# Seven-product part of an encoder kernel: VectorE's 128x2048 subtractions as two of 128x1024 each

## The chip, the cores and the metric

One core of a Trainium2 chip runs the whole kernel. The metric is the device time of one execution in microseconds (us). Three executions of the kernel before took 3186.99, 3185.45 and 3185.02 us; the median is 3185.45 us.

## The reference, cut to what matters

The model is an encoder of two layers over two sequences of 16 meta tokens and 512 tokens, with 1024 channels: one attention mixer, one state-space mixer, and a feed-forward block behind each. The change lies in the second feed-forward block:

```
def swiglu(u, w_gate, w_up, w_down):
    return (jax.nn.silu(u @ w_gate) * (u @ w_up)) @ w_down
# u = rmsnorm(h, ffn_norm[layer]);  h = h + swiglu(u, ...)
# w_gate, w_up: 1024 x 2816, w_down: 2816 x 1024, all float32
```

## The kernel before, in words

Every float32 product is made of three products of the shorter type fp32r: high part by high part, high weight by low token part, and low weight by high token part. A low part is the exact value minus the high part. The high part is a copy into fp32r.

The gate and up products of the second feed-forward block are cut into 2x2 blocks: two halves of the 1024 input channels (4 tiles of 128 each, `KH` = 4), two tiles of 128 outputs, and two halves of the tokens (512 each). For all but the first two tiles of gate and up, seven block products are made in place of eight (Strassen's scheme in Winograd's form). Each takes 4 x 3 = 12 matmuls of 128x128 by 128x512. The seven token operands are four plain or already turned halves and sums and differences of them; they are made once. The weight factors are made anew for each of the 20 pairs of output tiles (`PRODUCT_PAIRS`). The list `PRODUCTS` gives the order: (0,1), (0,2), (0,6), (0,5), (0,7), (1,1), (0,4), (0,3), (1,2), and so on; the first number is the pair and the second the product. We call them by their place in the list, t = 0, 1, 2, ...

The order on each engine is written out by hand, and semaphores tie the engines together:

- VectorE (DVE) makes the token operands: `first_difference` and `second_difference` per tile of 128x512; the third difference (line 3332) over 128x2048; the low parts of operands 2, 1 and 3 with `low_operand` (line 3267), 128x2048 each; `fourth_difference`, which is four steps of 128x512 (helper line 3241), a wait for the last of them, and one subtraction of 128x2048 (line 3262); two steps of the plain second hidden tile (lines 3340 and 3343, 128x1024); and the low part of operand 4 (line 3267 again). Behind them in its order stand the `take_quadrant` calls, which take finished products out of PSUM (lines 3277 and 3279).
- ScalarE (ACT) makes the high parts of the operands (`high_operand`, line 2353), the high parts of the weight factors (`high_factor`, line 2367), copies some products out of PSUM for later use (`tap`, line 2385) and applies silu (`quadrant_silu`, line 2390). Its order around t = 3 and 4 is: `high_factor(7)`, the high part of operand 4, silu of quadrant 0 of pair 0, `high_factor(8)`, `tap(4)`.
- GpSimd (POOL) makes the low parts of the weight factors (`low_factor`, line 999) and, ahead of the low factor of each product 6, four sums of weight quarters (`factor_sums`, lines 1006 to 1012). All are 128x512.
- TensorE (PE) runs `factor_product(t)`. It waits for the low factor t; for product 6, 5, 7 and 4 of pair 0 for `t_ready` 1, 2, 3 and 4, which the `low_operand` calls of VectorE give in that order; and for the taps (`tapped`) and the emptied banks (`quad_taken`). Product 4 of pair 0 (t = 6) needs `t_ready` 4 and `tap(4)`.
- SyncE (SP) issues the loads of the weight quarters, each when its old content has been used.

Of the kernel before, what the change touches and what calls it, by code (L numbers as in the profile page):

```python
# [22 lines left out]
F32 = mybir.dt.float32  # L23
F32R = mybir.dt.float32r
I32 = mybir.dt.int32
ALU = mybir.AluOpType
# [103 lines left out]
KH = KD // 2  # L130
# [193 lines left out]
def encoder(nc, tensors):  # L324
# [5 lines left out]
    def sb(name, shape, dt=F32, stack=None):  # L330
        return (stack or base).enter_context(nc.sbuf_tensor(name, shape, dt))
# [70 lines left out]
    with ExitStack() as s:  # L402
# [4 lines left out]
        with ExitStack() as s2:  # L407
            T1, T2, T3 = (sb(n, [P, 2, KH, SEQ], F32R, s2) for n in ("T1", "T2", "T3"))
        with ExitStack() as s2:
            TF1, TF2, TF3 = (sb(n, [P, 2, KH, SEQ], F32, s2) for n in ("TF1", "TF2", "TF3"))  # L410
# [103 lines left out]
    def real_half(ap, s):  # L514
        return ap[:, s * L + N_META:(s + 1) * L]

    def turned_half(ap):

        return ap[:, 0:KH, L + N_META:2 * L]
# [72 lines left out]
    b11_ready, t1_made, t2_made, t3_made = (Again(x, HEADS) for x in (k_hi, k_lo, q_hi, q_lo))  # L592
    t4_made, t_high = Again(q_turned, HEADS), Again(qs_ready, HEADS)
    t_ready, third_taken = Again(k_squared, HEADS), Again(kr_taken, HEADS)
# [1855 lines left out]
    def _(vec):  # L2450
# [59 lines left out]
        def step(ins):  # L2510

            ins.then_inc(vec_steps, c.adds(vec_steps))
            vec.wait_ge(vec_steps, c.given(vec_steps))
# [7 lines left out]
        for m in range(KQ + KKV):  # L2521
# [14 lines left out]
            if m >= KQ:  # L2536
                k = m - KQ
# [616 lines left out]
        for n in range(SCAN + 1):  # L3154
            i, k = divmod(n, CPS)
# [83 lines left out]
        def turned(dst, k, of, sub):  # L3239

            return vec.scalar_tensor_tensor(dst, of, col("ffn1", k), sub, ALU.mult, ALU.subtract)
# [13 lines left out]
        def fourth_difference():  # L3255

            f = turned_half(UF[1])
            vec.wait_ge(t_ready.sem, t_ready.at(1))
            for k in range(KH):
                ins = turned(f[:, k, :], KH + k, real_half(H[:, KH + k, :], 0), T2[:, 0, k, :].bitcast(F32))  # L3260
            step(ins)
            vec.tensor_tensor(f, f, T2[:, 1].bitcast(F32), ALU.subtract).then_inc(t4_made.sem, 1)

        def low_operand(n, hi, exact, lo):

            vec.wait_ge(t_high.sem, t_high.at(n))
            vec.tensor_tensor(lo, exact, hi.bitcast(F32), ALU.subtract).then_inc(t_ready.sem, 1)

        def take_quadrant(p, q):

# [22 lines left out]
        def add_down(m, g, final):  # L3293
# [35 lines left out]
        vec.sem_inc(third_taken.sem, 1)  # L3329
        vec.sem_inc(gate_ready, 1)  # L3330
        vec.wait_ge(t2_made.sem, t2_made.at(KH))
        vec.tensor_tensor(TF3[:, 1], TF2[:, 1], TF3[:, 1], ALU.subtract)\
            .then_inc(t3_made.sem, 1)
        low_operand(2, T2[:, 0], TF2[:, 1], T2[:, 1])
        low_operand(1, T1[:, 0], TF1[:, 1], T1[:, 1])
        low_operand(3, T3[:, 0], TF3[:, 1], T3[:, 1])
        vec.wait_ge(to_vector[0], c.want(to_vector[0]))
        fourth_difference()
        vec.wait_ge(plain_out.sem, plain_out.at(16))
        step(vec.tensor_tensor(hid_, real_group(0), rms, ALU.mult))  # L3340
# [200 lines left out]
```

## Time and profile before

| | |
|---|---|
| median of 3 executions | 3185.45 us |
| profiled execution | 3184.64 us |
| its span, first to last instruction | 3182.8 us |
| mean granted TensorE clock | 0.991 |
| PE busy | 3083.6 us, 97% |
| DVE busy | 1794.4 us, 56% |
| POOL busy | 1349.3 us, 42% |
| ACT busy | 916.5 us, 29% |

The span is the time between the first and the last instruction in the trace; 1.84 us of the profiled execution lie around it. Busy shares are averages over the whole span. A start in the rows is in us from the span's start, and durations include the time in which an instruction that has begun waits for something inside its engine.

### The profile page before, as it was taken

The page shows a single profiled execution, that of the slowest core. Times are in us where ns is not written, and L with a number is a line of the kernel's source. Part 1 is how long each engine was busy: PE and PEld are TensorE (multiplying, and loading weights), DVE is VectorE, ACT ScalarE, POOL GpSimd, SP SyncE. Part 2 cuts the span into 40 slices and gives each one's busy share as a digit, 9 for nine tenths or more (in the row PEclk, how much of TensorE's full clock was granted, in tenths as well). Part 3 has the DMA queues.
Part 4 walks back from the last instruction along what each step waited for, and adds up shares of the span by engine and source line. Part 5 has one row for each costly group of instructions (what it writes and reads, how often), then busy time and mean ns, then how long its engine had stood idle before and what let it go on. Part 6 is the DMA issues. An engine that isn't in the chain of part 4 may idle for free.

```text
span 3182.8 us, 46973 instructions
## 1 busy us (share of the span) xinstructions
PE 3083.6 (97%) x18566; PEld 2788.0 (88%) x18566; DVE 1794.4 (56%) x2496; ACT 916.5 (29%) x1628; POOL 1349.3 (42%) x710
## 2 busy tenths in 40 slices
PE   8999999899999999999999999899999899999997
PEld 8999999899999999999999988576667688887886
DVE  6677777643333333334788852588888833334334
ACT  4466665621000000001121122233334433332101
POOL 4100000133444444444444444467673577775442
PEclk9999999999999999999999999999999999999998
DMA  3011000121111111111243423332324122223221
GB/s 122 25 36 32 22 25 16 41 88 40 47 46 46 41 44 46 46 46 47 70 132 90 137 87 111 110 118 89 118 89 130 48 87 82 80 80 129 99 86 67
DMA packets 133065, 230.27 MB, mean 72 GB/s; under 512 B 10005, under 2 KB 59413, under 8 KB 132885
## 3 DMA queue, kind: packets, MB, share of 16 engines
q1 hardware_dynamic: 93136, 180.21, 16.7%
q10 hardware_dynamic: 39749, 47.60, 4.5%
q8 instruction: 121, 1.98, 0.3%
q14 instruction: 59, 0.48, 0.0%
HBM read 180.77 MB, written 46.99 MB: 72 GB/s over the span
## 4 chain that ended last, share of the span: by engine, by line
PE 84%; DVE 6%; POOL 5%; issue 4%; ACT 1%; DMA 0%; DVEq 0%; ACTq 0%; POOLq 0%
PE PS L1035 77%; PE PS L1289 4%; PE PS L1274 2%; POOL Wlo L915 1%; POOL SQ L960 1%; POOL RMS L925 1%; POOL SQ L955 1%; PE PS L1575 1%; DVE MX L2682 1%; DVE GD L3064 0%; POOL STB L947 0%; DVE XW L3026 0%; PE PS L1723 0%; DVE KAP L3069 0%; DVE YC L2931 0%
## 5 line engine op out<-in xcount | busy, mean ns | idle before, releaser
L870 POOL TENSOR_TENSOR Whi<-Wraw,const 128x1024 fp32r<-128x1024 f32 x145 | 354.7, 2446 | 1520.4 <-PE PS L1035 921.8
L1035 PE MATMUL PS<-Uhi,Whi 128*128 128x352 f32 (+1 forms) x2280 | 567.5, 341 | 17.1 <-DVE Ulo L2474 14.0
L1035 PE MATMUL PS<-Ulo,Whi 128*128 128x352 f32 (+1 forms) x2280 | 563.4, 339 | 0.0
L1035 PE MATMUL PS<-Uhi,Wlo 128*128 128x352 f32 (+1 forms) x2280 | 561.8, 339 | 0.0
L1035 PEld LDWEIGHTS PS<-Uhi,Whi 128*128 128x128 f32 x2280 | 395.0, 189 | 40.0 <-issue 17.4
L1035 PEld LDWEIGHTS PS<-Uhi,Wlo 128*128 128x128 f32 x2280 | 398.4, 189 | 20.8
L1035 PEld LDWEIGHTS PS<-Ulo,Whi 128*128 128x128 f32 x2280 | 397.6, 188 | 20.9
L873 POOL TENSOR_TENSOR Wlo<-Wraw,Whi 128x1024 fp32r<-128x1024 f32 x145 | 397.4, 2740 | 11.4
L1035 PE MATMUL PS<-T,Whi 128*128 128x512 f32 x768 | 225.7, 395 | 0.8 <-DVE HID L3285 0.5
L2815 DVE TENSOR_TENSOR H<-H,PS 128x1056 f32<-128x1056 f32 x88 | 110.3, 1253 | 130.7 <-PE PS L1035 130.6
L2931 DVE SCALAR_TENSOR_TENSOR YC<-XC,cols,YC 128x1052 f32<-128x1052 f32 (+1 forms) x96 | 180.8, 1884 | 3.4
L2682 DVE TENSOR_REDUCE MX<-PS 106x1 f32<-106x528 f32 x160 | 113.2, 707 | 113.0 <-PE PS L1035 112.3
L1035 PEld LDWEIGHTS PS<-T,Whi 128*128 128x128 f32 x768 | 143.8, 187 | 36.7 <-issue 0.9
L1289 PE MATMUL PS<-V,PT 106*106 106x64 f32 x1600 | 170.0, 254 | 0.5 <-ACT O L2017 0.5
L1289 PEld LDWEIGHTS PS<-V,PT 106*106 106x106 f32 x1600 | 161.8, 173 | 0.6 <-issue 0.6
L2112 ACT ACTIVATE HIDhi<-HID 128x1056 fp32r<-128x1056 f32 x20 | 21.8, 1088 | 457.1 <-DVE HID L2844 457.1
L2839 DVE TENSOR_TENSOR HID<-PS,RMS 128x1056 f32<-128x1056 f32 x22 | 27.7, 1258 | 217.7 <-PE PS L1035 217.4
L2006 ACT ACTIVATE PR<-PS,MX,TOK 106x528 f32<-106x528 f32 x160 | 126.5, 791 | 49.2 <-DVE MX L2685 48.9
L3296 DVE TENSOR_TENSOR H<-H,PS 128x1024 f32<-128x1024 f32 x47 | 57.4, 1220 | 141.3 <-PE PS L1035 141.3
L1035 PE MATMUL PS<-T,Wlo 128*128 128x512 f32 x384 | 136.0, 395 | 0.0
L999 POOL TENSOR_TENSOR Wlo<-Wraw,Whi 128x512 fp32r<-128x512 f32 x80 | 110.3, 1381 | 54.1 <-ACT Whi L2367 54.1
L1035 PE MATMUL PS<-YThi,Whi 128*128 128x512 f32 x256 | 120.7, 471 | 1.4 <-DVE Wlo L3151 0.8
(355 smaller groups left out, 6156.2 us busy)
## 6 DMA issues: line engine op xcount, KB each, us to landing
Wraw<-in_w SPq DMA_DIRECT2D x151, 512.0 KB, 3.2
Wraw<-in_w SPq DMA_DIRECT2D x152, 256.0 KB, 2.9
xt<-XTT ACTq DMA_DIRECT2D x20, 640.0 KB, 5.9
H<-in_x ACTq DMA_DIRECT2D x16, 528.0 KB, 8.3
zt<-ZB ACTq DMA_DIRECT2D x32, 256.0 KB, 2.1
X<-xt SPq DMA_DIRECT2D x8, 1024.0 KB
Z<-zt SPq DMA_DIRECT2D x32, 256.0 KB, 2.7
KFB<-keyf SPq DMA_DIRECT2D x15, 530.0 KB, 3.8
```

What stands on the lines that cost most here:

```text
L870: pool.tensor_tensor(Whi[s][:], Wraw[s][:], ones.unsqueeze(1).broadcast_to([P, BLK, P]), ALU.mult)\
L873: pool.tensor_tensor(Wlo[s][:], Wraw[s][:], Whi[s][:].bitcast(F32), ALU.subtract)\
L915: pool.tensor_tensor(Wlo[s][:], Wraw[s][:], Whi[s][:].bitcast(F32), ALU.subtract)\
L999: pool.tensor_tensor(OPLO[j % SLOTS], FACTOR[PRODUCTS[j][1]], OPHI[j % SLOTS].bitcast(F32), ALU.subtract)\
L1035: ins = pe.matmul(out, lhsT, rhs, start=start, stop=stop, skip_group_check=True)
L1274: ins = pe.transpose(PS[0:CW, A_TURN + b // TURN_DVE, b % TURN_DVE * CW:(b % TURN_DVE + 1) * CW], PR[t % 2][:, key_start(b):key_start(b) + ...
L1289: ins = pe.matmul(PS[0:CW, A_OUT, 0:VD], PT[t % 2][:, b, :], V[x // 4 % 2][:, n // KB * KB + b, x // 2 % 2, x % 2 * VD:(x % 2 + 1) * VD], ...
L2006: act.activation(PR[t % 2][:].rearrange("p (h n) -> p h n", h=2), PS[0:CW, A_SCORE:A_SCORE + 2, 0:QHALF], ACT.Exp, bias=MX[:, t % RING:t % ...
L2682: step(vec.tensor_reduce(MX[:, t % RING:t % RING + 1], PS[0:CW, A_SCORE:A_SCORE + 2, 0:QHALF], AX_XY, ALU.max))
L2815: ins = vec.tensor_tensor(h, h, of(g), ALU.add)
L2931: ins = vec.scalar_tensor_tensor(y_[:, :, to], x[:, :, of], taps[:, tap:tap + 1], y_[:, :, to], ALU.mult, ALU.add)
L3296: ins = vec.tensor_tensor(real(H[:, m, :]), real(H[:, m, :]), real_group(g), ALU.add)
```

## The change

Each of the five VectorE subtractions of 128x2048 becomes two of 128x1024. The first handles tiles 0 and 1 and the second tiles 2 and 3 of the four. The semaphore is given by the second. Nothing is moved, and no wait is added or removed.

```
         def fourth_difference():
             ...
             step(ins)
-            vec.tensor_tensor(f, f, T2[:, 1].bitcast(F32), ALU.subtract).then_inc(t4_made.sem, 1)
+            for k in range(0, KH, 2):
+                ins = vec.tensor_tensor(f[:, k:k + 2, :], f[:, k:k + 2, :], T2[:, 1, k:k + 2, :].bitcast(F32), ALU.subtract)
+            ins.then_inc(t4_made.sem, 1)
 
         def low_operand(n, hi, exact, lo):
             vec.wait_ge(t_high.sem, t_high.at(n))
-            vec.tensor_tensor(lo, exact, hi.bitcast(F32), ALU.subtract).then_inc(t_ready.sem, 1)
+            for k in range(0, KH, 2):
+                ins = vec.tensor_tensor(lo[:, k:k + 2, :], exact[:, k:k + 2, :], hi[:, k:k + 2, :].bitcast(F32), ALU.subtract)
+            ins.then_inc(t_ready.sem, 1)
...
-        vec.tensor_tensor(TF3[:, 1], TF2[:, 1], TF3[:, 1], ALU.subtract)\
-            .then_inc(t3_made.sem, 1)
+        for k in range(0, KH, 2):
+            ins = vec.tensor_tensor(TF3[:, 1, k:k + 2, :], TF2[:, 1, k:k + 2, :], TF3[:, 1, k:k + 2, :], ALU.subtract)
+        ins.then_inc(t3_made.sem, 1)
         low_operand(2, T2[:, 0], TF2[:, 1], T2[:, 1])
         low_operand(1, T1[:, 0], TF1[:, 1], T1[:, 1])
         low_operand(3, T3[:, 0], TF3[:, 1], T3[:, 1])
```

`low_operand` is called four times, so with the third and the fourth difference five instructions become ten.

## Rows read from the trace of the kernel before

**Rows 1.** The page: busy time of PE, and the chain's shares by engine.

```profile
PE 3083.6 (97%) x18566; PEld 2788.0 (88%) x18566; DVE 1794.4 (56%) x2496; ACT 916.5 (29%) x1628; POOL 1349.3 (42%) x710
PE 84%; DVE 6%; POOL 5%; issue 4%; ACT 1%; DMA 0%; DVEq 0%; ACTq 0%; POOLq 0%
```

**Rows 2.** Chain that ended last, 2480 to 2600: start us, us, what.

```profile
2502.79 0.50 POOL Wlo L999
...
2519.50 1.68 POOL OPS L999
...
2521.22 12.80 PE PS L1035 x48
2534.02 0.87 issue
```

**Rows 3.** Timeline of TensorE: start us, us, engine, line, what [idle before <-releaser].

```profile
2514.98 0.40 PE L1035 MATMUL PS<-Uhi,Wlo 128*128 128x512 f32 x1
2521.22 4.42 PE L1035 MATMUL PS<-T,OPS 128*128 128x512 f32 x12 [5.85 <-POOL OPS L999]
```

**Rows 4.** Timeline of GpSimd, 2502 to 2536.

```profile
2502.79 3.44 POOL L999 TENSOR_TENSOR Wlo<-Wraw,Whi 128x512 fp32r<-128x512 f32 x1 [13.54 <-ACT Whi L2367]
2509.49 3.35 POOL L1006 TENSOR_TENSOR S<-Wraw 128x512 f32<-128x512 f32 x1
...
2519.46 1.71 POOL L999 TENSOR_TENSOR OPS<-Wraw,OPS 128x512 fp32r<-128x512 f32 x1
2522.81 3.34 POOL L999 TENSOR_TENSOR Wlo<-Wraw,Whi 128x512 fp32r<-128x512 f32 x1
2526.10 3.54 POOL L999 TENSOR_TENSOR Wlo<-Wraw,Whi 128x512 fp32r<-128x512 f32 x2
2529.61 3.34 POOL L999 TENSOR_TENSOR OPS<-S,OPS 128x512 fp32r<-128x512 f32 x1
2534.39 1.28 POOL L999 TENSOR_TENSOR Wlo<-Wraw,Whi 128x512 fp32r<-128x512 f32 x1 [1.43 <-ACT Whi L2367]
```

**Rows 5.** Timeline of VectorE, 2498 to 2533.

```profile
2498.83 1.41 DVE L3241 SCALAR_TENSOR_TENSOR TF<-H,cols,TF 128x512 f32<-128x512 f32 x2
2500.16 1.23 DVE L3326 TENSOR_TENSOR HID<-HID,SILU 128x1024 f32<-128x1024 f32 x1
2501.31 1.22 DVE L3328 TENSOR_TENSOR GATE<-PS,RMS 128x1024 f32<-128x1024 f32 x1
2502.77 2.29 DVE L3332 TENSOR_TENSOR TF<-TF 128x2048 f32<-128x2048 f32 x1 [0.24 <-DVE GATE L3328]
2504.98 10.01 DVE L3267 TENSOR_TENSOR T<-TF,T 128x2048 fp32r<-128x2048 f32 x3
2514.91 6.80 DVE L3241 SCALAR_TENSOR_TENSOR UF<-H,cols,T 128x512 f32<-128x512 f32 x4
2521.75 3.25 DVE L3262 TENSOR_TENSOR UF<-UF,T 128x2048 f32<-128x2048 f32 x1
2524.92 1.21 DVE L3340 TENSOR_TENSOR HID<-PS,RMS 128x1024 f32<-128x1024 f32 x1
2526.28 2.21 DVE L3343 TENSOR_TENSOR HID<-HID,SILU 128x1024 f32<-128x1024 f32 x1
2528.64 3.16 DVE L3267 TENSOR_TENSOR Ulo<-UF,Uhi 128x2048 fp32r<-128x2048 f32 x1
2531.72 0.68 DVE L3277 TENSOR_TENSOR PS<-GATE,PS 128x512 f32<-128x512 f32 x1
```

**Rows 6.** Timeline of ScalarE, 2523 to 2535.

```profile
2523.75 1.15 ACT L2367 ACTIVATE Whi<-Wraw 128x512 fp32r<-128x512 f32 x2 [3.72 <-DMA Wraw<-in_w]
...
2526.69 1.91 ACT L2353 ACTIVATE Uhi<-UF 128x2048 fp32r<-128x2048 f32 x1
2533.16 0.63 ACT L2390 ACTIVATE GATE<-GATE 128x512 f32<-128x512 f32 x1 [4.56 <-DVE GATE L3279]
...
2534.22 0.58 ACT L2385 ACTIVATE SILU<-PS 128x512 f32<-128x512 f32 x1
```

**Rows 7.** Windows of 1 us: length, busy by engine, PEclk (granted clock), DMA.

```profile
2523.00:2524.00 1.00, 1.00 (x4) 0.71 (x3) 1.00 (x1) 0.25 (x1) 1.00 (x1) 0.50 0.11 41
2534.00:2535.00 1.00, 0.13 (x2) 0.14 (x2) 0.10 (x1) 0.79 (x2) 0.61 (x1) 1.00 0.00 0
```

**Rows 8.** Waits of TensorE from 2536 on: total us, times, longest.

```profile
PE PS L1035 <- DVEq L3382: 2.7, 1, 2.7
PE PS L1035 <- ACT SQ L2431: 1.1, 2, 0.6
```

## The prediction

> **What bounds the kernel now.** I read the page first. TensorE is busy for 97% of the span and carries 84% of the chain that ended last [rows 1], so a change to VectorE can only count where TensorE stands idle. The chain in order of time shows two such places near the edited lines. It leaves TensorE at about 2502.8, runs over GpSimd's low factors and sums until 2521.2, goes back to TensorE for 48 matmuls (t = 2 to 5), and has a hole of 0.87 us at 2534.0 which it calls "issue" [rows 2]. TensorE's timeline gives the first place its size: the last matmul of t = 1 starts at 2514.98 and lasts 0.40, and t = 2 starts at 2521.22, after 5.85 us of idleness that GpSimd's low factor 2 ended [rows 3].
>
> Next I read GpSimd and VectorE side by side, since both are busy without a break there. A GpSimd subtraction of 128x512 takes 1.28 us alone (at 2534.39) but 3.44, 3.35 and 3.34 us beside VectorE's 128x2048 instructions, and 1.71 beside its 128x512 ones [rows 4]. VectorE is slowed in turn: its first 128x2048 instruction takes 2.29 us, the three that follow 10.01 together; its 128x512 steps go from 1.41 for two to 6.80 for four, and a 128x1024 product of two SBUF tensors from 1.23 to 2.21 [rows 5]. The two take turns, one instruction each. From start to start, a 128x2048 instruction has 2504.98 - 2502.77 = 2.21 us alone and (2514.91 - 2504.98)/3 = 3.31 with a GpSimd turn in it, a 128x512 step about (2500.16 - 2498.83)/2 = 0.67 and 6.84/4 = 1.71. A GpSimd turn thus costs VectorE 1.04 to 1.10 us, whatever the size of its own instruction. VectorE's line 3340, which reads PSUM and one SBUF tensor, takes 1.21 beside GpSimd and was not held up [rows 4, 5].
>
> The Trainium skill, SBUF — State Buffer, "Who interferes with whom", says that a VectorE instruction with two SBUF inputs and a GpSimd instruction that reads SBUF exclude each other for a whole instruction, that one with a single SBUF input does not take part, and that it is the order of issue, not the shape, that decides who blocks. The trace agrees with the first two (2.29 against 3.31 us; line 3340 with 1.21). The advice in its summary to favour whichever side is on the critical path speaks against this change if VectorE is the later side; that is what the next step looks into.
>
> **The hole at 2534.0 is VectorE's.** Product t = 6 needs `tap(4)`, which is the ScalarE copy at 2534.22 of 0.58 us; it ends at 2534.80, and TensorE starts at 2534.89 (2534.02 + 0.87) [rows 2, 6]. That copy stands behind `high_factor(8)`, which stands behind the silu of quadrant 0 at 2533.16, which had waited 4.56 us for VectorE's line 3279 [rows 6]. Line 3279 and 3277 (start 2531.72) are `take_quadrant(0, 0)`, right behind the low part of operand 4 [rows 5]. From 2502.77 to 2531.72 VectorE runs without a gap over 0.15 us [rows 5]. So there are two gates: GpSimd's chain ends at 2521.2, VectorE's at 2531.7, and the second already ends last.
>
> **The change, gate by gate.** *GpSimd's gate (gain).* Seven GpSimd instructions lead to low factor 2: two low factors, four sums, low factor 2. Now they wait for the VectorE turns TF, three low operands and three 128x512 steps: 4 x 2.21 + 3 x 0.67 = 10.85 us. With halves they wait for seven half turns. A 128x1024 instruction alone takes 2501.31 - 2500.16 = 1.15 us from start to start [rows 5], so 7 x 1.15 = 8.05. Low factor 2 is ready 2.8 us earlier, at about 2518.4, and TensorE's idleness falls from 5.85 to about 3.0 us. The four products t = 2 to 5, of 12.80 us [rows 2], then end at about 2531.2 instead of 2534.0.
>
> *VectorE's gate (loss).* The halves give GpSimd more turns before VectorE is through. Before, ten VectorE instructions of this stretch hold a GpSimd turn: the three low operands, four 128x512 steps, the fourth difference, line 3343, and the last low operand (the long ones in rows 5). GpSimd has 12 instructions up to low factor 7; the other two are free, one beside line 3340, one (at 2529.61) after VectorE's last [rows 4]. With halves I lay them out again: turns behind TF's first half and so on, seven until low factor 2 (2518.4); low factor 3 before the first 128x512 step, 4 to 6 before the other three, 7 before the first half of the fourth difference. All 12 now fall on VectorE instructions with two SBUF inputs. Low factors 5 and 6 need quarters that are reloaded after low factor 2; now ScalarE has them at 2523.75 [rows 6], 2.6 us after 2521.2, so then at about 2521.0, in time for a turn at 2522.3. Low factor 7 needs t = 2 done, at about 2518.4 + 4.4 = 2522.8, in time for 2526. Low factor 8 can't come early: its high part stands behind the silu. So two more turns at 1.05 = 2.1 us. Each split costs 2 x 1.15 - 2.21 = 0.09, five times 0.45 us. VectorE's gate moves by 2.1 + 0.45 = 2.55 us, from 2531.72 to about 2534.3. The high part of operand 4 (1.91 us) is covered by lines 3340 and 3343, 1.36 + 1.15 = 2.51 us. Everything behind it (silu, `high_factor(8)`, `tap(4)`) follows, and t = 6 starts at 2534.89 + 2.55 = 2537.4.
>
> *TensorE's clock (loss).* TensorE then idles from 2531.2 to 2537.4, 6.2 us, where it idled 0.87 us. After the 5.85 us of idleness the granted clock was 0.50, that is 1.2 GHz, up to 2524 at least, and t = 2 took 4.42 us [rows 3, 7]; 12 matmuls at the full clock take (12.80 - 4.42)/36 x 12 = 2.8 us. That is 1.6 us lost. After 0.87 us the clock stayed at 1.00 [rows 7]. The first idleness still lasts 3.0 us and the clock may fall in it as before; its loss lies ahead of the second gate and is hidden. The new long one comes right ahead of t = 6, whose 1.6 us nobody hides.
>
> *Behind t = 6.* TensorE waits for nothing longer than 2.7 us until the end, and that at the final norm [rows 8]; GpSimd's next low factor hangs on ScalarE and moves along. The delay is passed on whole.
>
> Sum: 2.55 + 1.6 = 4.2 us slower. Against the profiled execution: 3184.64 + 4.2 = 3188.8. It was 0.8 us below the median of the three; on the median, 3185.45 + 4.2 = 3189.6 us. The gain of 2.8 us at the first gate is worth nothing, since the later gate moves the other way.
>
> Bounds. The number of added turns is 1 to 3 (a low factor that misses its turn and runs beside line 3340 is free; one more can't be excluded): 1.05 to 3.15 us. The split costs 0 (if the second half starts as if it were one instruction) to 0.45. The clock costs 0 to 1.6. So the mechanism gives +1.1 to +5.2.
>
> **Rivals.** (a) *Gain stays.* If t = 6 is not held by VectorE, the 2.8 us of the first gate are kept and the hole of 0.87 may close: 3181.8 to 3182.7 us. It decides if `take_quadrant(0, 0)` begins by 2531.72 - 3.7 = 2528.0. Half of the chain's view speaks for it: the profile names only the first gate and calls the second "issue". Against it: VectorE has no gap to give up, and splitting removes no work. (b) *The change doesn't do what it says.* Both halves may run with no GpSimd turn between them, as the second one is already queued when the first ends. Then GpSimd's turns stay, and the time is +0 to 0.45: 3185.7. Against it: today the three low operands are queued as closely, and a GpSimd turn stands between each two. (c) *Turns, but no clock loss*: 3185.45 + 2.55 = 3188.0. Against it stands the fall in 5.85 us of idleness. (d) *Something larger*: the reordered turns push a low factor behind its product in pair 1 as well, with another idle stretch and another 1.6 us: +7 or more, 3192.5 or later. GpSimd's low factor 9 is done about 1 us ahead of its product, but both move by the same amount.
>
> **How the numbers follow.** Forecast 0.58, (a) 0.12, (b) 0.12, (c) 0.13, (d) 0.05. The forecast alone spans 3187.5 to 3190.9. The range, 3184.8 to 3191.5, takes in (b) and (c) and leaves out (a) and (d). A change within 0.2% (6.4 us), about what a measurement of this kernel can tell from no change, is by far the likeliest, since all cases but (d) stay within it: slower by over 0.2% 0.05, faster 0.02, same 0.93.
>
> **What would show it.** Right: GpSimd's 128x512 instructions of about 2.3 us in place of 3.35 from 2503 on; TensorE idle about 3 us ahead of t = 2; line 3277 first at about 2534.3; TensorE idle some 6 us ahead of t = 6 and its first 12 matmuls at half the clock. Wrong: line 3277 at or before 2531.7, GpSimd durations as before, or a full clock at t = 6. A change of more than 6.4 us either way would mean that I missed a stage.

## The result, and the profile after

The changed kernel takes 3189.89 us (median of 20 executions, 3187.03 to 3195.63), the kernel before 3184.37 us in 20 executions beside it. The ratio is 1.0018, with a 95% interval of 1.0012 to 1.0024: slower by about 5.5 us (3.8 to 7.6). The forecast was 3189.6 us, 4.2 us slower. In one later set of runs three executions of the kernel before took 3498 to 6131 us; they are left out of its median there.

All times below that are "from the third difference" count from the start of its first instruction. This takes out what earlier stages add by chance: that start lay at 2502.77 us before, 2505.21 in the profile after, and 2502.43 in another profile of the same changed kernel. The profiled execution after has a span of 3190.4 us, so it shows 7.6 us more than before, of which 2.44 lie ahead of the edited lines.

VectorE's timeline of the changed kernel answers to [rows 5]:

```profile
2505.21 3.46 DVE L3337 TENSOR_TENSOR TF<-TF 128x1024 f32<-128x1024 f32 x2 [0.25 <-DVE GATE L3332]
2508.60 13.49 DVE L3270 TENSOR_TENSOR T<-TF,T 128x1024 fp32r<-128x1024 f32 x6
2522.02 6.85 DVE L3241 SCALAR_TENSOR_TENSOR UF<-H,cols,T 128x512 f32<-128x512 f32 x4
2528.90 3.33 DVE L3263 TENSOR_TENSOR UF<-UF,T 128x1024 f32<-128x1024 f32 x2
2532.15 1.21 DVE L3345 TENSOR_TENSOR HID<-PS,RMS 128x1024 f32<-128x1024 f32 x1
2533.51 1.22 DVE L3348 TENSOR_TENSOR HID<-HID,SILU 128x1024 f32<-128x1024 f32 x1
2534.65 2.35 DVE L3270 TENSOR_TENSOR Ulo<-UF,Uhi 128x1024 fp32r<-128x1024 f32 x2
2536.92 0.69 DVE L3281 TENSOR_TENSOR PS<-GATE,PS 128x512 f32<-128x512 f32 x1
```

The six halves of the low operands take 13.49 us where the three whole ones took 10.01. The last row starts 31.71 us after the first (28.95 before): VectorE is 2.76 us later. The hidden step at 2533.51 and the last low operand are short now (1.22 and 2.35 us, before 2.21 and 3.16), because GpSimd has nothing left to do by then. GpSimd's timeline, which answers to [rows 4], shows it:

```profile
2505.23 4.60 POOL L999 TENSOR_TENSOR Wlo<-Wraw,Whi 128x512 fp32r<-128x512 f32 x2 [12.90 <-ACT Whi L2367]
2512.17 2.16 POOL L1008 TENSOR_TENSOR Wraw<-Wraw 128x512 f32<-128x512 f32 x1
...
2518.77 2.24 POOL L999 TENSOR_TENSOR OPS<-Wraw,OPS 128x512 fp32r<-128x512 f32 x1
...
2528.28 1.73 POOL L999 TENSOR_TENSOR OPS<-S,OPS 128x512 fp32r<-128x512 f32 x1
2539.60 1.27 POOL L999 TENSOR_TENSOR Wlo<-Wraw,Whi 128x512 fp32r<-128x512 f32 x1 [9.59 <-ACT Whi L2367]
```

Its instructions take about 2.2 to 2.3 us in place of 3.35, and low factor 7 (at 2528.28) comes ahead of the fourth difference instead of running on behind low operand 4. Then it idles for 9.59 us. TensorE's timeline answers to [rows 3]:

```profile
2521.06 4.60 PE L1035 MATMUL PS<-T,OPS 128*128 128x512 f32 x12 [4.29 <-POOL OPS L999]
...
2533.65 0.40 PE L1035 MATMUL PS<-Uhi,Wlo 128*128 128x512 f32 x1
2540.10 0.77 PE L1035 MATMUL PS<-Uhi,Whi 128*128 128x512 f32 x1 [6.05 <-ACT SILU L2385]
2540.67 0.63 PE L1035 MATMUL PS<-Ulo,Whi 128*128 128x512 f32 x1
```

From the third difference, t = 2 starts at 15.85 us (before 18.45) and t = 6 at 34.89 us (before 32.12). The gain of 2.6 us at GpSimd's gate is there, and it is lost in the 6.05 us of idleness ahead of t = 6. After that the clock is at half, as windows of 1 us show (columns as in [rows 7]):

```profile
2539.00:2540.00 1.00, 0.00 (x0) 0.00 (x0) 0.00 (x0) 1.00 (x2) 0.40 (x1) 0.50 0.00 0
...
2544.00:2545.00 1.00, 1.00 (x4) 0.72 (x3) 0.00 (x0) 0.08 (x1) 0.92 (x2) 0.50 0.00 0
...
2546.00:2547.00 1.00, 1.00 (x6) 0.83 (x5) 0.29 (x1) 1.00 (x4) 1.00 (x2) 1.00 0.00 0
```

The granted clock is 0.50 (1.2 GHz) from 2539 into 2545, and t = 6 runs 0.43 us from matmul to matmul in place of 0.23. The chain of waits now names what ends last, where before it had only "issue" [rows 2]:

```profile
2534.65 2.35 DVE Ulo L3270 x2
2537.01 0.62 DVE PS L3281
2537.65 0.70 DVE GATE L3283
2538.39 0.07 issue
2538.48 0.42 issue
2538.91 0.61 ACT Whi L2367
2539.52 0.49 ACT SILU L2385
2540.01 0.09 issue
2540.10 60.10 PE PS L1035 x247
```

It runs through VectorE's low operand 4, the emptying of quadrant 0, and ScalarE's silu (the two "issue" pieces), high factor 8 and tap. The last row also sizes the clock's loss in this profile: 247 matmuls take 60.10 us, where the 280 of before took 65.19, that is 57.5 us for 247. The difference is 2.6 us.

A second mark, the first matmul of the final norm, shows what has arrived there. Here it is before and after:

```profile
3156.30 1.05 PE L1035 MATMUL PS<-const,SQ 128*128 128x1 f32 x8 [0.59 <-ACT SQ L2431]
```

```profile
3163.98 1.05 PE L1035 MATMUL PS<-const,SQ 128*128 128x1 f32 x8 [0.53 <-ACT SQ L2431]
```

From the start of t = 6 to this mark it takes 3156.30 - 2534.89 = 621.41 us before and 3163.98 - 2540.10 = 623.88 us after, 2.47 us more. With the 2.77 us ahead of t = 6 that makes 5.24 us. In the other profile of the changed kernel (e11 below) the two parts are 2.79 and 1.49 us, 4.28 in all. Both sums lie within the interval of the medians' 5.5 us.

### The profile page after: what moved, and what is told of

Read it like the earlier page. It is cut to its first block, busy times and chain, and to the rows that moved or that the text cites. A ratio compares the mean times of both kernels' runs of the same rounds, so it can differ in the third digit from the quotient of the medians.

```text
span 3190.4 us, 46979 instructions
## 1 busy us (share of the span) xinstructions
PE 3090.0 (97%) x18566; PEld 2793.9 (88%) x18566; DVE 1796.6 (56%) x2502; ACT 917.7 (29%) x1628; POOL 1344.0 (42%) x710
## 4 chain that ended last, share of the span: by engine, by line
PE 83%; DVE 7%; POOL 4%; issue 4%; ACT 1%; DMA 0%; DVEq 0%; ACTq 0%; POOLq 0%
PE PS L1035 76%; PE PS L1289 4%; PE PS L1274 2%; POOL Wlo L915 1%; POOL SQ L960 1%; POOL RMS L925 1%; DVE MX L2682 1%; POOL SQ L955 1%; PE PS L1575 1%; DVE GD L3064 0%; POOL STB L947 0%; PE PS L1723 0%; DVE XW L3026 0%; DVE T L3270 0%; ACT PR L2006 0%
```

## The experiments

Medians are of 11 or 12 executions each, given as the difference from the kernel before, which ran on the same chip (15 to 33 executions). e1 to e4 ran on one chip, e5 to e8 on a second, e9 to e11 on a third and e12 on a fourth, so where runs of different chips are compared it is by these differences. The intervals of the ratios are about 0.09% (3 us) to either side, so device times tell steps of 3 us and more, and single steps are read in the trace, from the third difference. A table behind e11 has both marks for every run.

**e2 and e3: which halves do it.** e2 halves the third difference and low operands 2, 1 and 3; e3 the other two.

```
         def low_operand(n, hi, exact, lo):
             ...
-            for k in range(0, KH, 2):
+            n_ = 2 if n in (1, 2, 3) else KH     # e3: n in (4,)
+            for k in range(0, KH, n_):
             ...
```

> Halves for the third difference and the low operands 2, 1 and 3; the fourth difference and low operand 4 stay whole. Theory (turns): GpSimd gets all its extra turns in this front part, so the same two extra turns as in the changed kernel stand before line 3277; two splits of 0.09 us fewer. From the third difference's start to t = 6: 34.7 us (34.9 changed, 32.1 before); device time as the changed kernel within 0.5 us. Rival (0.55 us per extra instruction): three fifths to four fifths of the shift, 34.3 us. Rival (the back halves are what delays line 3277): 32.1 us and the time of before.

Measured: t = 6 at 34.75 us, device time +4.2 us (ratio 1.0015, 1.0006 to 1.0024).

```profile
2518.27 3.05 PE L1035 MATMUL PS<-T,OPS 128*128 128x512 f32 x12 [3.30 <-POOL OPS L999]
...
2537.21 0.76 PE L1035 MATMUL PS<-Uhi,Whi 128*128 128x512 f32 x1 [7.50 <-ACT SILU L2385]
```

The third difference starts at 2502.46 in this profile. The idle stretch ahead of t = 2 shrinks to 3.30 us and the one ahead of t = 6 grows to 7.50: the front halves alone give the change's whole delay at t = 6.

> Halves for the fourth difference and low operand 4 only; the third difference and low operands 2, 1, 3 whole. Theory (turns): low factor 4, which ran free beside the PSUM step, now falls between the two halves of the fourth difference: one extra turn of 1.05 us and two splits of 0.09, so t = 6 starts at 33.3 us after the third difference's start (32.1 before, 34.9 changed), and the start of t = 2 is as before, 18.4 us. TensorE idles about 2.1 us ahead of t = 6; whether the clock falls there is open, so the device time is 1.2 to 3.8 us over before. Rival (0.55 us per extra instruction): 33.2 us, no help in telling the two apart by the total, but then low factor 4's duration would stay at 3.3 us; turns says about 2.3. Rival (the front halves alone cause it): 32.1 us.

Measured: t = 2 at 18.42 us, t = 6 at 33.33 us, after 1.21 us of idleness (not 2.1: the clock stayed low for longer in t = 2, so TensorE came later). The clock did not fall again. Device time +0.2 us (0.9991 to 1.0009), below the 1.2 us that I expected at least; a step of 1.2 us is inside that interval. So the back halves alone delay t = 6 by 1.2 us, and beside the front halves they add 0.1 (34.89 against 34.75): GpSimd's 12 instructions are used up by then. What tells turns from a price for each instruction is low factor 4, which took 3.34 us before [rows 4]:

```profile
2525.30 2.27 POOL L999 TENSOR_TENSOR Wlo<-Wraw,Whi 128x512 fp32r<-128x512 f32 x1
```

**e1: quarters.** The same edit in all three places:

```
-            for k in range(0, KH, 2):
+            for k in range(0, KH):
```

> The five subtractions in four instructions of 128x512 each (20 in place of 10). I measure from the start of the first instruction of the third difference to the start of product t = 6: 32.1 us before, 34.9 us after the change. Theory (turns): only GpSimd's 12 instructions can take a turn before the last low operand is through, and in the changed kernel all 12 already do. So quarters add no turn against the changed kernel, only the cost of starting: 4 x 0.67 - 2.30 = 0.4 us per subtraction, 1.9 us in all, giving 36.8 us; GpSimd's first gate (start of t = 2) comes 3 us earlier than in the changed kernel, at about 12.6 to 13 us. Rival (each extra VectorE instruction costs the same 2.8/5 = 0.55 us, whatever GpSimd does): 15 extra against before, 8.3 us, giving 40.4 us. In device time: turns 2 us over the changed kernel, rival 5.5 us over it.

Measured: t = 6 at 36.05 us, device time +4.2 us (1.0007 to 1.0025), the same as e2's. Doubling the instructions once more adds 1.2 us, not 5.5. The rival with a price for each instruction is out. The timeline shows why: once GpSimd's 12 turns are used up, VectorE's 128x512 instructions run at their own speed.

```profile
2507.91 17.12 DVE L3270 TENSOR_TENSOR T<-TF,T 128x512 fp32r<-128x512 f32 x12
2524.96 2.73 DVE L3241 SCALAR_TENSOR_TENSOR UF<-H,cols,T 128x512 f32<-128x512 f32 x4
2527.72 2.50 DVE L3263 TENSOR_TENSOR UF<-UF,T 128x512 f32<-128x512 f32 x4
```

The four steps at 2524.96 take 2.73 us, against 6.80 before [rows 5]. The cost of starting was overrated: a plain 128x512 subtraction takes 2.41/4 = 0.60 us from start to start (low operand 4, no turn in it), not the 0.67 of the steps with a column factor.

**e5: the changed kernel, GpSimd held back.** All VectorE instructions are as in the change; only waits are added on GpSimd.

```
         for j, (p, k) in enumerate(PRODUCTS):
             ...
+            if j == 5:
+                pool.wait_ge(t4_made.sem, t4_made.at(1))
+            if j == 6:
+                pool.wait_ge(t_ready.sem, t_ready.at(4))
             low_factor(j)
```

> The changed kernel, all VectorE instructions as they are; only GpSimd waits longer: low factor 5 for the fourth difference, low factors 6 and 7 for low operand 4. Theory (turns): three of the 12 GpSimd turns leave the stretch ahead of line 3281 (low factor 5 runs beside the PSUM step, 6 and 7 behind the last low operand, in time for t = 6). So t = 6 starts 3 x 1.05 = 3.15 us earlier, 31.7 us after the third difference's start (changed kernel 34.9, before 32.1), with TensorE idle some 3 us ahead of it. Device time 3 us or more below the changed kernel's. Rival (a cost of each VectorE instruction, not of GpSimd's turns): VectorE's stretch stays at 31.7 us, t = 6 at 34.9.

Measured: t = 6 at 31.84 us, device time +0.2 us (0.9993 to 1.001), against +5.0 for the changed kernel (e11, on another chip). TensorE idles 3.01 us ahead of t = 6 and the clock stays at 1.00, so e5 takes away the clock's loss as well as the turns. VectorE's rows with their three missing turns:

```profile
2519.89 4.79 DVE L3245 SCALAR_TENSOR_TENSOR UF<-H,cols,T 128x512 f32<-128x512 f32 x4
2524.70 2.36 DVE L3267 TENSOR_TENSOR UF<-UF,T 128x1024 f32<-128x1024 f32 x2
...
2531.77 0.69 DVE L3285 TENSOR_TENSOR PS<-GATE,PS 128x512 f32<-128x512 f32 x1
```

The four steps take 4.79 us (6.85 in the changed kernel) and the two halves of the fourth difference 2.36 (3.33). That is 2.06 + 0.97 = 3.03 us for three turns. With nothing changed on VectorE, this settles that t = 6 is late by GpSimd's turns.

**e4: TensorE kept busy.**

```
                 pe.wait_ge(low_made.sem, low_made.at(t + 1))
+                if t == 6:
+                    for n in range(25):
+                        mm(PS[:, 2, :], OPHI[t % SLOTS][:, 0:P], T1[:, 0, n % KH, :])
```

> The changed kernel with 25 extra matmuls of 128x512 into an unused PSUM bank ahead of t = 6, 5.8 us of work where TensorE idled 6.05 us. Theory (the idle stretch lets the clock fall to half, and that costs 2.6 us behind it): t = 6 starts as in the changed kernel, 34.9 us after the third difference's start, the granted clock stays 1.00 through it, its 12 matmuls take 2.8 us in place of about 5.1, and the device time is 2.0 to 2.8 us less than the changed kernel's. Rival (the clock loss is hidden or unimportant, VectorE's 2.8 us and something else explain the difference): the time stays that of the changed kernel or rises.

Measured: t = 6 at 34.84 us as in the changed kernel, but at full clock, and device time +1.7 us (0.9996 to 1.0014), 3.3 below the +5.0 of e11 on another chip. On its own chip it is 2.5 below e2, which has nearly the same t = 6 with the clock fall; all 11 executions of e4 (3185.48 to 3188.38) are shorter than all 11 of e2 (3188.70 to 3192.49).

```profile
2538.03 0.50 PE L1035 MATMUL PS<-Uhi,Whi 128*128 128x512 f32 x1 [0.18 <-ACT SILU L2388]
2538.37 0.39 PE L1035 MATMUL PS<-Ulo,Whi 128*128 128x512 f32 x1
```

The window behind it (columns as in [rows 7]) has the clock at 1.00:

```profile
2539.00:2541.00 2.00, 2.00 (x10) 1.62 (x10) 0.51 (x1) 0.00 (x0) 1.92 (x2) 1.00 0.00 0
```

From the start of t = 6 to the final norm it takes 621.39 us, as before (621.41); the changed kernel takes 623.88 and 622.90 us in its two profiles. So the fall costs 2.5 us in one and 1.5 in the other. The clock is low for 6.8 us in both. In the profile after it falls at 2538.8, 1.3 us ahead of t = 6, and 5.5 us of work run at half; in e11 it falls at 2533.8, 3.6 us ahead of t = 6 (2537.34), and 3.3 us of work do.

**e6: GpSimd's gate alone taken away, from the kernel before.**

```
+        pool.wait_ge(t2_made.sem, t2_made.at(2))
+        factor_sums(0, (0, 1))
         for j, (p, k) in enumerate(PRODUCTS):
             if k == 6:
-                factor_sums(p)
+                factor_sums(p, (0, 1, 2, 3) if p else (2,))
             low_factor(j)
+            if j == 2:
+                factor_sums(0, (3,))
```

> The kernel before (128x2048 throughout) with two of GpSimd's four sums of pair 0 made ahead, beside VectorE's PSUM steps before the third difference, and the fourth sum behind low factor 2. Only four turns lead to t = 2, which starts about 13.3 us after the third difference's start in place of 18.4: TensorE's first idle stretch is all but gone. Theory (VectorE's gate ends last): t = 6 moves by one turn only, to 31.2 us, and TensorE's idleness moves there, 5 to 6 us, with a clock fall behind it that costs up to 2.6 us: device time 0 to 2 us ABOVE before, although 5 us of idleness ahead of t = 2 are gone. Rival (GpSimd's chain, the one that the profile's chain names, is the bound): 5 us faster than before.

Measured: device time +1.8 us (0.9998 to 1.0016); its profiled execution (span 3183.0) had started the third difference 1.4 us early, and from there to the final norm it takes 1.7 us more than before.

```profile
2514.76 3.06 PE L1039 MATMUL PS<-T,OPS 128*128 128x512 f32 x12 [1.74 <-POOL OPS L999]
...
2532.60 0.77 PE L1039 MATMUL PS<-Uhi,Whi 128*128 128x512 f32 x1 [5.35 <-ACT SILU L2389]
```

From 2501.39, t = 2 starts at 13.37 us and t = 6 at 31.21. Of the 5.85 us of idleness that the chain of before named, 4.1 went away ahead of t = 2, and it brought no time: t = 6 is 0.9 us earlier, but 5.35 us of idleness stand ahead of it, with a clock fall.

**e7: quadrant 0 emptied earlier, from the kernel before.**

```
         fourth_difference()
+        take_quadrant(0, 0)
         ...
         for p in range(PRODUCT_PAIRS):
-            take_quadrant(p, 0)
+            if p:
+                take_quadrant(p, 0)
```

> The kernel before with the emptying of quadrant 0 of pair 0 (two PSUM steps, 1.4 us) moved from behind low operand 4 to behind the fourth difference. Theory: the silu, high_factor(8) and tap(4) no longer wait for VectorE's end; t = 6 then waits for low operand 4 alone, which ends at about 30.4 us, 1.4 later than before, and for TensorE's own products until 31.25 us. t = 6 starts at 31.3 us in place of 32.1; device time 0.9 us below before. Rival (low operand 4 itself is what t = 6 waits for): t = 6 starts 1.4 us later than before, 33.5 us.

Measured: +0.2 us (0.9993 to 1.001). TensorE has no wait ahead of t = 6 any more (36 matmuls follow t = 2 without a break), though VectorE's low operand 4 ends 1.2 us later than before. But t = 2 took 5.40 us in place of 4.42, since the low clock lasted longer there, and t = 6 started at 32.0 us. The 0.9 us are not seen; the part about what t = 6 waits for is.

**e8 and e12: both gates moved.** e6's edit, quadrant 0 emptied right behind low operand 3 and no longer behind low operand 4, and low factor 7 held back:

```
+            if j == 7:
+                pool.wait_ge(t_ready.sem, t_ready.at(4))
             low_factor(j)
...
         low_operand(3, T3[:, 0], TF3[:, 1], T3[:, 1])
+        take_quadrant(0, 0)
```

> From the kernel before: the two sums ahead as in e6, quadrant 0 emptied right behind low operand 3, low factor 7 held until low operand 4. Theory: both gates move together. t = 2 starts at about 13.3 us after the third difference's start, t = 6 at about 27.3 us (before 32.1), no idle stretch of TensorE over 2 us and no clock fall; device time about 4.8 us below before. Rival (VectorE is made later by waiting for the tap of product 0, or the sums made ahead push the third difference itself back): less than 2 us gained, or none.

> The rearranged kernel e8 a second time, since its first interval just touched 1. Theory: t = 6 at 27.3 us after the third difference's start, no clock fall in this stretch, device time 3 to 5 us below before. Rival (the first measurement was a lucky draw): within 1.5 us of before.

Measured: -4.0 us (0.9982 to 1.0) and, the second time, -3.0 us (0.9982 to 1.0). In e8's profile (third difference at 2501.06):

```profile
2514.43 3.06 PE L1041 MATMUL PS<-T,OPS 128*128 128x512 f32 x12 [1.73 <-POOL OPS L999]
...
2520.80 0.70 PE L1041 MATMUL PS<-T,Whi 128*128 128x512 f32 x2 [0.33 <-issue]
...
2528.40 0.47 PE L1041 MATMUL PS<-Uhi,Whi 128*128 128x512 f32 x1 [1.78 <-DVE Ulo L3273]
...
2537.63 0.73 PE L1041 MATMUL PS<-T,Whi 128*128 128x512 f32 x2 [0.67 <-POOL Wlo L999]
```

t = 6 starts at 27.34 us (27.35 the second time), 4.8 earlier than before, and the clock stays up throughout this stretch. About 0.9 us of this is lost again ahead of the final norm, 0.67 of them in a new wait for a low factor (last row); 3.8 us (3.9 the second time) arrive there. This version has a lower median than both kernels twice; each interval by itself reaches up to 1.

**e9 and e10: are halves of use once both gates are moved?** e9 is e8 with all five subtractions in halves, e10 with the third difference and low operand 2 only.

```
-            vec.tensor_tensor(lo, exact, hi.bitcast(F32), ALU.subtract).then_inc(t_ready.sem, 1)
+            for k in range(0, KH, 2):             # e10: whole unless n == 2
+                ins = vec.tensor_tensor(lo[:, k:k + 2, :], ...)
+            ins.then_inc(t_ready.sem, 1)
```

> The rearranged kernel e8 with all five subtractions in halves, as in the change. Theory (turns): even where both gates have been moved, the halves give GpSimd two more turns ahead of low operand 4's end and cost five splits: t = 6 starts 2.0 to 2.8 us later than in e8 (27.3 us), at 29.3 to 30.1 us after the third difference's start; with the longer idle stretch a clock fall is likely. Device time 2 to 5 us above e8. Rival (with VectorE's gate relieved the earlier first gate pays): t = 6 earlier than in e8, device time below it.

> e8 with halves for the third difference and low operand 2 only. Low factor 2 then comes before TensorE asks for it, so t = 2 has no idle stretch in front. Theory (turns): one more GpSimd turn falls on a VectorE instruction with two SBUF inputs, so t = 6 starts at about 28.6 us, 1.2 later than in e8, and the time is 1 to 3 us above e8's. Rival: the 1.7 us of idleness ahead of t = 2 are gained.

Measured: t = 6 at 29.14 us (e9) and 28.72 (e10) against 27.34 in e8; both with a clock fall (idle 6.29 and 4.33 us ahead of t = 6); device times -0.9 and -1.6 us against before, 1.4 to 3.1 us above e8's two. At the final norm e9 is 2.6 us and e10 2.4 us later than e8. Even here the halves move idleness from t = 2 to t = 6 and add to it. e9 came out 0.2 us below the range expected for t = 6, because the halves added one turn and not two: the three low operands and the third difference hold seven turns in place of three, but the four steps behind them take 3.69 us with one turn (5.75 with three in e8), and the fourth difference has none (one in e8). That makes 8 turns against 7.

**e11: the changed kernel again.** No edit.

> The changed kernel itself once more, on the chip of the other two, as the standard for e1 to e5. All theories: t = 6 starts 34.9 us after the third difference's start, idle 6 us ahead of it, and the device time is 4 to 5.5 us over before.

Measured: t = 6 at 34.91 us, +5.0 us (1.0011 to 1.0029), idle 7.64 us ahead of t = 6 (the clock had not fallen at t = 2 here, so t = 2 took 3.06 us and TensorE was through earlier).

**All runs at both marks.** Times are in us. The first column of numbers is the start of t = 6 from the third difference, the second goes from there to the final norm's first matmul, and the third is their sum as a difference from before. The last column is the difference of the medians of device time.

| run | t = 6 | t = 6 to final norm | sum, against before | device time, against before |
|---|---|---|---|---|
| before | 32.12 | 621.41 | | |
| changed | 34.89 | 623.88 | +5.2 | +5.5 |
| e11, changed | 34.91 | 622.90 | +4.3 | +5.0 |
| e1, quarters | 36.05 | 623.19 | +5.7 | +4.2 |
| e2, front halves | 34.75 | 622.96 | +4.2 | +4.2 |
| e3, back halves | 33.33 | 621.15 | +1.0 | +0.2 |
| e4, TensorE kept busy | 34.84 | 621.39 | +2.7 | +1.7 |
| e5, GpSimd held back | 31.84 | 621.34 | -0.4 | +0.2 |
| e6, sums ahead | 31.21 | 624.03 | +1.7 | +1.8 |
| e7, quadrant 0 earlier | 32.04 | 621.34 | -0.2 | +0.2 |
| e8, both gates | 27.34 | 622.35 | -3.8 | -4.0 |
| e12, e8 again | 27.35 | 622.28 | -3.9 | -3.0 |
| e9, e8 in halves | 29.14 | 623.18 | -1.2 | -0.9 |
| e10, e8 with two in halves | 28.72 | 623.39 | -1.4 | -1.6 |

The two last columns agree within 1.5 us. The rest of the span, from the final norm's first matmul to the end, differs from profile to profile without a link to the edits that I can name: 25.2 to 27.5 us, with 26.4 in the profile after and 27.5 in e11 for the same kernel.

## Why the prediction was right

**GpSimd's gate.** Forecast: t = 2 earlier by 2.8 us, idle 3.0 us ahead of it. Measured: 2.6 us from the third difference; idle 4.29 us in the profile after and 3.31 in e11. The first is longer because TensorE itself came from its plain column earlier, which no step of the forecast covered.

**VectorE's gate.** Forecast: two more turns and five splits, 2.55 us, line 3277's counterpart at 31.5 us. Measured: 31.71 us, 2.76 later. The count was right: all 12 GpSimd instructions stood ahead of the fourth difference's second half, and low factor 7 was where the layout had put it. e5 removed three turns and got 3.03 us back, e2 showed that the front halves are enough for the whole delay, and e1 that the number of instructions does not set it. The Trainium skill, SBUF — State Buffer, "Who interferes with whom", has the rule behind it: a VectorE instruction with two SBUF inputs and a GpSimd instruction that reads SBUF exclude each other for a whole instruction. The turns that e5 took away agree. So does the step that reads PSUM and one SBUF tensor: it took 1.21 us beside GpSimd before [rows 5] and 1.21 us after, at 2532.15, where GpSimd was idle.

**TensorE's clock.** Forecast: 1.6 us, sized by the restart at t = 2 before [rows 3, 7]. Measured: 2.5 us in the profile after, 1.5 us in e11. The term was right in one and too small in the other, and it also stood as its own upper bound, which was too tight. In the profile before, the clock had fallen 1.9 us into the idle stretch, and 2.9 us of work ran at half. In the profile after, it fell 4.7 us into it, and 5.5 us of work did; in e11 it was 3.3 us. One row could not show how much that varies.

**The rivals.** Rival (a), the gain stays, fell with the first trace and with e6: 4.1 us of idleness taken out ahead of t = 2 brought no time. Rival (b), no turn between the halves, fell with GpSimd's durations (2.3 us, not 3.35). Rival (c), no clock loss, fell with e4. Rival (d), low factors late in pair 1, did not occur: behind t = 6 the changed kernel's waits of TensorE are those of before.

**The sum, and some luck.** The mechanism's bound of 5.2 us is just short of the 5.5 us between the medians, whose interval is 3.8 to 7.6; the two traces have 5.2 and 4.3 us. The forecast of 3189.6 us lies only 0.3 us from the median measured, but that closeness is luck: it started from a median of three executions, 3185.45 us, that was 1.1 us above the median of 20, and its step was 1.3 us too small.

## What to carry to other kernels

Where VectorE instructions with two SBUF inputs run beside GpSimd instructions that read SBUF, the two engines alternated here instruction by instruction, so cutting the instructions of one gives the other more turns: it speeds up the second at the price of the first, for as long as the second has instructions left. Ask which of the two is waited for last before cutting, and count the turns up to that point. An idle stretch that the chain of waits names can be followed by a hidden one that is nearly as late: look at how much slack the next gate has before working on the first. And an idle stretch of TensorE should be weighed with the clock behind it: those of 5.35 to 7.64 us ahead of t = 6 (e6, e1, e2 and the changed kernel) cost 1.5 to 2.6 us more than themselves, where nothing hid it.

## What the runs showed of the hardware

- A GpSimd turn of 128x512 costs VectorE about 1 us (0.97 to 1.10) beside instructions of 512, 1024 and 2048 elements alike. In e1, 12 subtractions of 128x512 with 9 turns between them take 17.05 us from start to start, 9 x 1.09 + 12 x 0.60.
- The clock did not fall with every idle stretch of TensorE. After 3.30 us ahead of t = 2 in e2, 3.01 us ahead of t = 6 in e5 and 1.78 us in e8 it stayed at 1.00. Within 5.35 us (e6) and 4.33 us (e10) it fell. With 4.29 us ahead of t = 2 in the profile after and 3.79 us in e4 and e5 it fell only after the restart, when t = 2 had run for 0.7 to 0.9 us. In the profiles where it fell during the idleness the granted clock was 0.50 for 6.8 us (before, e3 and e7 around t = 2; e1, e2, e6, e9, e10 and the changed kernel around t = 6); in those where it fell after the restart, for 3.4 us (profile after, e4 and e5 around t = 2).
- The stretch ahead of the edited lines differs by up to 4 us from profile to profile (third difference at 2501.06 to 2505.28 us; 2502.43 and 2505.21 for the changed kernel alone), which is as much as the changes studied here. Counting from a fixed instruction near the edit gave starts of t = 6 that repeat: 34.89 and 34.91 us for the changed kernel, 27.34 and 27.35 for e8's.
